# Zero products in front of the expert products' wait, in a streaming encoder step on one core

## Chip, cores and metric

The kernel runs on one core of a Trainium2 chip. The metric is the device time of one execution in microseconds (us), as the median over runs. The program is written engine by engine: TensorE (PE, whose weight loads the profile lists as PEld), VectorE (DVE), ScalarE (ACT), GpSimd (POOL) and SyncE (SP) each have their own instruction list, and semaphores order them.

## What is computed

One inference step of a one-layer trunk over 1,024 prompt tokens and 32 sample tokens, all in fp32, model width 1,024. Cut to what matters here:

```
h  = x + W_out . concat(RMSNorm(StickBreaking(q, k, v)), RMSNorm(SinkWindowGQA(q, k, v)))
h' = h + PEER(RMSNorm(h));   y = RMSNorm(h')

peer_ffn(x):                                   # 8 heads, 16 experts each, of 16384
    q = x @ w_q;  s1 = q1 . keys_1;  s2 = q2 . keys_2
    v1, i1 = top_k(s1, 16);  v2, i2 = top_k(s2, 16)
    best, pos = top_k(v1 + v2, 16);  idx = chosen of i1 * 128 + i2;  gate = softmax(best)
    hid = gelu(u[idx] . x)
    y   = sum_k gate * hid * v[idx]            # rows of u and v are fetched by index
```

Each token fetches 128 rows of u and of v (4 KB each), so the expert rows are nearly all of the traffic from memory.

## The kernel before

The first phase (to about 60 us) projects the first tile of 128 tokens. All the rest is one fused phase, written as a list of slots, `for n in range(FIRST_SLOT, LAST_SLOT)`, which each engine walks in the same order. A slot is one gather: from slot 0 to slot 1,055 POOL starts one indirect DMA (L975) that brings 128 rows of u and v, 8 KB each, into one of the eight places of the ring `uv`. Slots 0 to 1,055 cover 33 groups of 32 tokens.

The work of a slot pair (a batch) passes through four engines. DVE multiplies the u half with the tokens and sums (`dot`, L1195). ACT applies Gelu (L1115) and makes two diagonal matrices of gate times activation, `diag` (L1121); POOL prepares their gate part, `gate_fold` (L961). PE, in slot 2*batch+3, waits for the batch's diagonals and multiplies them with the v half (`experts`, L1733): four products of a 128x32 stationary tile with 512 moving columns, each into its own quarter of the partitions of the PSUM tile `y_acc`. The semaphore `vmm` then counts the gathers whose place in the ring is free, and POOL's gather n waits until n-7 of them are done (`hold(pool, S["vmm"], n - RING + 1)`).

Between these, tables of slots place the other work by hand. `STEP_AT` holds the steps of the stick-breaking attention: PE's `scores` (L1465) in the step's slot, `sums` (L1485, L1488, L1492) four slots later, `values` (L1512) eight slots later, with ACT's softplus and exponential and DVE's `keep` (L1211, L1217) between them. `WINDOW_AT`, `TAIL_AT`, `PRODUCT_AT` hold the window attention and the output projection (L1627), `ROUTE_AT` the routing of one head (queries L1668, L1676, L1682, selection L1703, with the top-k on DVE), `X_AT` the copies of tokens (L1654), `PAIR_AT` the folding of finished groups (L1716). Up to slot 216 or so PE also projects the remaining tokens (L1594). In each slot PE does `experts` first and the other work after it, in program order; nothing on PE overtakes a wait.

`y_acc` has two banks of 512 columns, and a group's products are summed in one of them from its first batch (`opens`, which sets `start=True`) to its last.

Of the kernel before, what the change touches and what calls it, by code (L numbers as in the profile page):

```python
# [13 lines left out]
P = 128  # L14
# [27 lines left out]
GT = 32  # L42
# [47 lines left out]
def hold(engine, sem, value):  # L90

    engine.wait_ge(sem, value)
    engine.nop(nofuse=True)
# [400 lines left out]
def steps_of(t):  # L494

    return 2 * blocks_of(t) if t < NT else blocks_of(t)
# [5 lines left out]
def route_slot(t, head):  # L502

    if t == 0:
        return 8 * head - 23
    if t == 1:
        return 88 + 10 * head
    return t * P - 62 + (14 if t < NT else 10) * head

def stretch(t):

    return 7 if t in STREAMED else 0

def tail_slot(t):

    return route_slot(t, 0) - 28 - stretch(t)

def window_slot(t, w):

    return tail_slot(t) - 20 + 4 * w

def step_slot(t, e):

    return window_slot(t, 0) - 6 - 4 * (steps_of(t) - e)
# [13 lines left out]
LATE_K_AT = {}  # L542
# [4 lines left out]
GATHERS = (NT + 1) * P - 3 * TS  # L547
# [5 lines left out]
STEP_AT = {step_slot(t, e): (t, e) for t in range(NT + 1) for e in range(steps_of(t))}  # L553
WINDOW_AT = {window_slot(t, w): (t, w) for t in range(NT + 1) for w in range(4)}
TAIL_AT = {tail_slot(t): t for t in range(NT + 1)}
TAIL_END_AT = {tail_slot(t) + stretch(t): t for t in range(NT + 1)}
PRODUCT_AT = {tail_slot(t) + 9 + k * (2 if t in STREAMED else 1): (t, k) for t in range(NT + 1) for k in range(DK)}
ROUTE_AT = {route_slot(t, head): (t, head) for t in range(NT + 1) for head in range(PH)}
# [3 lines left out]
PAIR_AT = {min(PT * (g + 1), GATHERS): g for g in range(NP)}  # L562
X_FIRST = [-10, -5, 12, 60, 98, 126, 168, 188]
X_AT = {}
# [3 lines left out]
FINISH_AT = {min((t + 1) * P, GATHERS): t for t in range(NT + 1)}  # L568

def fused_phase(nc, io, r):

    with ExitStack() as ctx:
        def sb(name, shape, dt=F32):
            return ctx.enter_context(nc.sbuf_tensor("f_" + name, shape, dt))
# [3 lines left out]
        w_q, w_out, ident, neg_suffix, neg_ones = r.w_q, r.w_out, r.ident, r.neg_suffix, r.neg_ones  # L579
# [42 lines left out]
        w_first = uv[:, 0:4, :].rearrange("p r (k n) -> p (r k) n", n=DM)  # L622
        w_stream = (part(4, 6), g_final[:])
        hid = sb("hid", [P, 8, 2])
        act_hid = sb("act_hid", [P, 4, 2])
        gate_fold = sb("gate_fold", [P, 3, 2, GT])
        diag = sb("diag", [P, 3, 2, GT])
# [3 lines left out]
        y_acc = ps("y_acc", [P, DM])  # L631
# [52 lines left out]
        def expert_of(n):  # L684

            pair, s = divmod(n, PT)
            head, s = divmod(s, 2 * PART if pair < NP - 1 else PART)
            j, rank = divmod(s, PART)
            g = 2 * pair + j
            return (g, g // GROUPS, g % GROUPS, head, rank)  # L690
# [258 lines left out]

        @block.gpsimd  # L950
        def _(pool):
            nc.gpsimd.memset(q_pad[:], 0.0).then_inc(S["zeroed"], 1)

            def spread_gates(batch):
                g, t, j, head, rank = expert_of(2 * batch)
                hold(pool, S["routed"], t * PH + head + 1)
                if batch >= 3:
                    pool.wait_ge(S["diag"], batch - 2)
                full = [P, 2, GT]
                k = j * PART + rank  # L960
                nc.gpsimd.tensor_tensor(gate_fold[:, batch % 3, :, :], fold[:].unsqueeze(1).broadcast_to(full),  # L961
                                        gates[:, head, k:k + 2].unsqueeze(2).broadcast_to(full),
                                        ALU.mult).then_inc(S["gate_fold"], 1)

            hold(pool, S["op"], 1)
            for n in range(GATHERS):
                if n < RING:
                    hold(pool, S["late_mm"], 2 * n + (2 if n < RING // 2 else 4))
                g, t, j, head, rank = expert_of(n)
                if rank == 0:  # L970
                    hold(pool, S["routed"], t * PH + head + 1)
                if n >= RING:
                    hold(pool, S["vmm"], n - RING + 1)
                k = j * PART + rank
                pool.indirect_dma_start(uv[:, n % RING, :], None, io["peer_uv"],  # L975
                                        bass.IndirectOffsetOnAxis(ap=idx[:, head, k:k + 1], axis=0),
                                        ).then_inc(S_UV[n % RING], 16)
                if n % 2 == 1:
                    spread_gates(n // 2)
# [471 lines left out]
        def _(pe):  # L1451
# [257 lines left out]
            def fold_pair(pair, b, n):  # L1709
# [7 lines left out]
                                            start=True, stop=True, skip_group_check=True)  # L1717
                last.then_inc(S["y_fold"], 1)

            def experts(batch):  # L1720
                g = expert_of(2 * batch)[0]
                opens = 2 * batch == FIRST_OF[g]
                pe.wait_ge(S["diag"], batch + 1)
                if opens and g >= 2:
                    pe.wait_ge(S["y_ev"], g - 1)
                if batch == 0:
                    pe.wait_ge(S["late_ev"], IN_Y)
                    pe.wait_ge(S["late_nat"], sum(u < IN_Y for u in LATE_NATURAL))
                for i in range(2):
                    n = 2 * batch + i  # L1730
                    for b in range(2):
                        quarter = slice((i + 2 * b) * GT, (i + 2 * b + 1) * GT)
                        last = nc.tensor.matmul(y_acc[quarter, g % 2 * 512:(g % 2 + 1) * 512], diag[:, batch % 3, i, :],  # L1733
                                                uv[:, n % RING, DM + b * 512:DM + (b + 1) * 512],
                                                start=opens, stop=False, skip_group_check=True)
                    last.then_inc(S["vmm"], 1)

            for n in range(FIRST_SLOT, LAST_SLOT):
                if n % 2 == 1 and 0 <= n - 3 < GATHERS:
                    experts(n // 2 - 1)  # L1740
# [89 lines left out]
```

## Time and profile before

| | |
|---|---|
| median of 3 runs | 3173.43 us (3172.75 to 3174.1) |
| the profiled execution's own time | 3165.28 us |
| its span, first to last instruction | 3163.4 us |
| PE busy | 2237.8 us, 71% |
| DVE busy | 2204.5 us, 70% |
| ACT, POOL busy | 49% each |
| mean granted TensorE clock | 0.797 of 2.4 GHz |
| moved by DMA | 1216.73 MB, 385 GB/s over the span |

### The profile page before, as it was taken

The page shows a single profiled execution, that of the slowest core. Times are in us where ns is not written, and L with a number is a line of the kernel's source. Part 1 is how long each engine was busy: PE and PEld are TensorE (multiplying, and loading weights), DVE is VectorE, ACT ScalarE, POOL GpSimd, SP SyncE. Part 2 cuts the span into 40 slices and gives each one's busy share as a digit, 9 for nine tenths or more (in the row PEclk, how much of TensorE's full clock was granted, in tenths as well). Part 3 has the DMA queues.
Part 4 walks back from the last instruction along what each step waited for, and adds up shares of the span by engine and source line. Part 5 has one row for each costly group of instructions (what it writes and reads, how often), then busy time and mean ns, then how long its engine had stood idle before and what let it go on. Part 6 is the DMA issues. An engine that isn't in the chain of part 4 may idle for free.

```text
span 3163.4 us, 42434 instructions
## 1 busy us (share of the span) xinstructions
PE 2237.8 (71%) x12346; PEld 1128.1 (36%) x12346; DVE 2204.5 (70%) x5717; ACT 1539.9 (49%) x3399; POOL 1544.9 (49%) x1596
## 2 busy tenths in 40 slices
PE   7978788688767756766577657767677666767663
PEld 4755334344333322332243223332333234432220
DVE  3268548684677767786777766786777767686886
ACT  2235325452257425753476337752677347753222
POOL 0034455354544555455555554455554644466553
PEclk9989889789877867887688778887788877767675
DMA  8379999899999999999999999999999999999997
GB/s 326 95 289 411 417 400 416 322 407 383 421 420 373 417 422 397 363 417 416 420 378 354 417 425 359 364 419 421 394 373 366 423 389 406 406 393 417 426 425 299
DMA packets 243623, 1216.73 MB, mean 385 GB/s; under 512 B 30528, under 2 KB 90304, under 8 KB 107200
## 3 DMA queue, kind: packets, MB, share of 16 engines
q0 software_dynamic: 152528, 1108.81, 85.4%
q1 hardware_dynamic: 90864, 105.22, 9.6%
q8 instruction: 99, 1.62, 0.2%
q14 instruction: 132, 1.08, 0.1%
HBM read 1197.56 MB, written 16.47 MB: 384 GB/s over the span
## 4 chain that ended last, share of the span: by engine, by line
DMA 30%; PE 27%; DVE 20%; issue 8%; DVEq 5%; ACT 3%; POOL 2%; ACTq 2%; SPq 0%; another core or an unknown queue 0%; POOLq 0%
DMA r_uv<-peer_uv,f_idx 27%; DVE r_uv L1195 8%; PE f_y_acc L1733 6%; PE f_q_ps L1668 4%; PE f_z L1627 3%; PE f_z L1485 3%; POOL r_uv L975 2%; PE f_z L1492 2%; PE f_y_acc L1594 2%; PE f_z L1465 2%; ACTq L1119 2%; DMA f_work<-w_out 1%; PE f_o_sb L1512 1%; PE f_o_sw L1654 1%; ACT f_diag L1121 1%
## 5 line engine op out<-in xcount | busy, mean ns | idle before, releaser
L975 POOL DMA_INDIRECT r_uv<-peer_uv,f_idx x1056 | 1270.1, 1203 | 1358.7 <-PE f_y_acc L1733 960.7
L1195 DVE CUSTOM_DVE_ANT_0 r_uv<-r_uv,r_x_rep 128x1024 f32<-128x1024 f32 x1056 | 1287.4, 1226 | 521.0 <-DMA r_uv<-peer_uv,f_idx 511.4
L1733 PE MATMUL f_y_acc<-r_uv,f_diag 128*32 128x512 f32 x4224 | 722.4, 760 | 689.7 <-ACT f_diag L1121 684.5
L1115 ACT ACTIVATE f_act_hid<-f_hid 128x2 f32<-128x2 f32 x528 | 107.3, 203 | 942.7 <-DVE f_hid L1195 916.2
L1733 PEld LDWEIGHTS f_y_acc<-r_uv,f_diag 128*32 128x32 f32 x4224 | 94.7, 119 | 972.1 <-ACT f_diag L1121 893.9
L988 ACT ACT_TABLE_LOAD x191 | 245.1, 1283 | 235.3 <-PE f_z L1465 168.7
L961 POOL TENSOR_TENSOR f_gate_fold<-r_fold,f_gates 128x64 f32<-128x64 f32 x528 | 269.0, 509 | 172.7 <-ACT f_diag L1121 157.3
L1115 ACT ACT_TABLE_LOAD x259 | 332.3, 1283 | 4.5
L1668 PE MATMUL f_q_ps<-r_w_q,f_xnT 128*128 128x256 f32 x1152 | 322.8, 429 | 9.7 <-ACT f_xnT L1084 5.8
L1121 ACT ACTIVATE f_diag<-f_gate_fold,f_act_hid 128x32 f32<-128x32 f32 x1056 | 281.9, 314 | 37.9 <-issue 1.7
L1668 PEld LDWEIGHTS f_q_ps<-r_w_q,f_xnT 128*128 128x128 f32 x1152 | 236.3, 214 | 101.1 <-issue 43.0
L1485 PE MATMUL f_z<-f_work,r_neg_suffix 128*128 128x512 f32 (+2 forms) x178 | 134.0, 847 | 73.6 <-DVE f_work L1217 51.1
L1512 PEld LDWEIGHTS f_o_sb<-f_work 128*128 128x128 f32 (+2 forms) x848 | 104.6, 187 | 20.2 <-ACT f_work L1020 10.2
L1627 PE MATMUL f_z<-r_w_out,f_work 128*128 128x512 f32 (+1 forms) x192 | 100.1, 665 | 13.2 <-DVE f_work L1282 13.2
L1512 PE MATMUL f_o_sb<-f_work 128*128 128x64 f32 (+2 forms) x848 | 105.3, 281 | 2.0 <-ACT f_work L1020 2.0
L1654 PE MATMUL f_o_sw<-r_ident,f_xnT 128*32 128x128 f32 x2112 | 92.5, 329 | 18.9 <-issue 13.7
L1465 PE MATMUL f_z<-f_q_pad,f_work 128*128 128x256 f32 x288 | 89.4, 440 | 16.8 <-DMA f_work<-scratch_projT 16.8
L1485 PEld LDWEIGHTS f_z<-f_work,r_neg_suffix 128*128 128x128 f32 (+1 forms) x178 | 37.8, 257 | 165.7 <-DVE f_work L1217 118.6
L1465 PEld LDWEIGHTS f_z<-f_q_pad,f_work 128*128 128x128 f32 x288 | 67.3, 237 | 78.4 <-issue 72.0
L1654 PEld LDWEIGHTS f_o_sw<-r_ident,f_xnT 128*32 128x32 f32 x2112 | 72.1, 133 | 58.6 <-issue 56.1
L1492 PE MATMUL f_z<-f_work,r_neg_ones 128*128 128x512 f32 (+1 forms) x144 | 91.0, 723 | 0.0
L1195 DVE DVE_READ_ACCUMULATOR2_ANT f_hid<- 128x1 f32 x1056 | 85.7, 81 | 0.0
(209 smaller groups left out, 2964.2 us busy)
## 6 DMA issues: line engine op xcount, KB each, us to landing
r_uv<-peer_uv,f_idx POOLq DMA_INDIRECT x1056
f_work<-scratch_projT SPq DMA_DIRECT2D x86, 128.0 KB
r_w_out<-w_blocks SPq DMA_DIRECT2D x36, 256.0 KB
f_work<-out_sb_v_prompt SPq DMA_DIRECT2D x72, 128.0 KB
r_uv<-w_blocks SPq DMA_DIRECT2D x16, 512.0 KB, 11.0
r_w_q<-w_peer_q SPq DMA_DIRECT2D x8, 1024.0 KB, 10.6
x_in<-x_prompt SPq DMA_DIRECT2D x8, 512.0 KB, 10.0
f_q_pad<-scratch_projT SPq DMA_DIRECT2D x64, 64.0 KB
```

Of the source, the lines that this page charges most:

```text
L961: nc.gpsimd.tensor_tensor(gate_fold[:, batch % 3, :, :], fold[:].unsqueeze(1).broadcast_to(full), gates[:, head, k:k + 2].unsqueeze(2).bro ...
L975: pool.indirect_dma_start(uv[:, n % RING, :], None, io["peer_uv"], bass.IndirectOffsetOnAxis(ap=idx[:, head, k:k + 1], axis=0),).then_inc( ...
L988: act.preload_act_table_set("natural_log_exp_and_others")
L1115: nc.scalar.activation(act_hid[:, batch % 4, :], hid[:, batch % 8, :], ACT.Gelu)
L1121: made = nc.scalar.activation(diag[:, batch % 3, i, :], gate_fold[:, batch % 3, i, :], ACT.Copy, scale=act_hid[:, batch % 4, i:i + 1])
L1195: nc.vector.tensor_tensor_reduce(row_u, row_u, x_rep[:, g % 3, :], 1.0, 0.0, ALU.mult, ALU.add, hid[:, n // 2 % 8, n % 2:n % 2 + 1]).then_ ...
L1465: last = nc.tensor.matmul(z[:, at:at + 256], kT[:, (e % 2) * 256 + m * P:(e % 2) * 256 + (m + 1) * P], q_pad[:, f, m, :, :].rearrange("p a ...
L1485: nc.tensor.matmul(out, neg_suffix[0:keys, 0:keys], sp[0:keys, 0:width], start=False, stop=False, skip_group_check=True)
L1512: last = nc.tensor.matmul(o_sb[0:n, hd * HD:(hd + 1) * HD], probs[0:keys, i * n:(i + 1) * n], block, start=(e == 0 and i == 0), stop=False ...
L1654: last = nc.tensor.matmul(o_sw[c * GT:(c + 1) * GT, k % 4 * P:(k % 4 + 1) * P], xnT[:, k, tokens], ident[:], start=True, stop=True, skip_g ...
L1668: last = nc.tensor.matmul(q_ps[:, 0:2 * QH], xnT[:, k, :], w_q[:, k, head * 2 * QH:(head + 1) * 2 * QH], start=(k == 0), stop=(k == DK - 1))
L1733: last = nc.tensor.matmul(y_acc[quarter, g % 2 * 512:(g % 2 + 1) * 512], diag[:, batch % 3, i, :], uv[:, n % RING, DM + b * 512:DM + (b + ...
```

## The change

A tile of zeros, 128x32, is cleared once by POOL. Before PE waits for a batch's diagonals it now issues a number of products with that zero tile as the stationary operand and `neg_ones`, repeated to 512 columns, as the moving one. They go into the first quarter of the bank in which the batch's group is being summed, so they add nothing. A batch that opens its bank gets none. How many there are is a table made when the program is built: `PE_WORK` adds up a cost in us for PE's work in each slot, and `FILL_AT[n]` is the number of products of cost 0.43 that fill the two slots n-2 and n-1 up to 3.0. It starts at slot 261. In all 590 products stand ahead of 191 of the 528 batches: one at 14 of them, two at 36, three at 60 and four at 81.

```diff
@@ -568,6 +568,25 @@
+PE_WORK = {n: 1.1 for n in range(3, GATHERS + 3, 2)}
+
+
+def count_work(table, offset, cost):
+
+    for slot in table:
+        PE_WORK[slot + offset] = PE_WORK.get(slot + offset, 0.0) + cost
+
+
+for table, offset, cost in ((STEP_AT, 0, 0.9), (STEP_AT, 4, 1.7), (STEP_AT, 8, 0.8), (WINDOW_AT, 0, 0.4), (WINDOW_AT, 4, 0.4),
+                            (WINDOW_AT, 6, 0.4), (TAIL_AT, 6, 0.9), (TAIL_END_AT, 24, 0.9), (PRODUCT_AT, 0, 1.7),
+                            (X_AT, 0, 1.0), (ROUTE_AT, 0, 1.7), (ROUTE_AT, 1, 1.7), (ROUTE_AT, 4, 0.3), (ROUTE_AT, 6, 0.5),
+                            (ROUTE_AT, 15, 0.3), (PAIR_AT, 4, 0.5), (PAIR_AT, 8, 0.5), (LATE_K_AT, 0, 0.9)):
+    count_work(table, offset, cost)
+FILL_TO, FILLER = 3.0, 0.43
+FILL_AT = {n: int((FILL_TO - PE_WORK.get(n - 2, 0.0) - PE_WORK.get(n - 1, 0.0)) / FILLER)
+           for n in range(2 * P + 5, GATHERS + 3, 2)}
@@ -622,6 +641,7 @@
+        zeros = sb("zeros", [P, GT])
@@ -949,6 +969,7 @@
         @block.gpsimd
         def _(pool):
+            nc.gpsimd.memset(zeros[:], 0.0)
             nc.gpsimd.memset(q_pad[:], 0.0).then_inc(S["zeroed"], 1)
@@ -1717,9 +1738,18 @@
+            def fill(n, g):
+
+                for _ in range(FILL_AT.get(n, 0)):
+                    nc.tensor.matmul(y_acc[0:GT, g % 2 * 512:(g % 2 + 1) * 512].rearrange("p (a c) -> p a c", a=4), zeros[:],
+                                     neg_ones[:].unsqueeze(1).broadcast_to([P, 4, P]), start=False, stop=False,
+                                     skip_group_check=True)
+
             def experts(batch):
                 g = expert_of(2 * batch)[0]
                 opens = 2 * batch == FIRST_OF[g]
+                if not opens:
+                    fill(2 * batch + 3, g)
                 pe.wait_ge(S["diag"], batch + 1)
```

The lists below name matmuls by line, output, operands and shape; L1763 of the changed kernel is L1733 of the one before, L1506 is L1485, L1513 is L1492, L1486 is L1465, L1533 is L1512, L1697 is L1676, L1703 is L1682, L1724 is L1703 and L1675 is L1654. The first place is PE's list in a stretch with attention steps, about 1921 to 1948 us of the trace (slots 609 to 615). Before:

```order
L1512 MATMUL f_o_sb<-f_work 128x64 x4
L1733 MATMUL f_y_acc<-r_uv,f_diag 32x512 x4
L1676 MATMUL f_q_ps<-r_ident,f_q 128x128 x2
L1733 MATMUL f_y_acc<-r_uv,f_diag 32x512 x4
L1485 MATMUL f_z<-f_work,r_neg_suffix 128x512
L1492 MATMUL f_z<-f_work,r_neg_ones 128x512
L1465 MATMUL f_z<-f_q_pad,f_work 128x256 x2
L1512 MATMUL f_o_sb<-f_work 128x64 x4
L1682 MATMUL f_q_ps<-r_keysT,f_q 128x128 x2
L1733 MATMUL f_y_acc<-r_uv,f_diag 32x512 x8
L1485 MATMUL f_z<-f_work,r_neg_suffix 128x512
```

The same place in the changed kernel:

```order
L1533 MATMUL f_o_sb<-f_work 128x64 x4
L1763 MATMUL f_y_acc<-r_uv,f_diag 32x512 x4
L1697 MATMUL f_q_ps<-r_ident,f_q 128x128 x2
L1744 MATMUL f_y_acc<-r_neg_ones,f_zeros 32x512 x3
L1763 MATMUL f_y_acc<-r_uv,f_diag 32x512 x4
L1506 MATMUL f_z<-f_work,r_neg_suffix 128x512
L1513 MATMUL f_z<-f_work,r_neg_ones 128x512
L1486 MATMUL f_z<-f_q_pad,f_work 128x256 x2
L1533 MATMUL f_o_sb<-f_work 128x64 x4
L1703 MATMUL f_q_ps<-r_keysT,f_q 128x128 x2
L1763 MATMUL f_y_acc<-r_uv,f_diag 32x512 x4
L1744 MATMUL f_y_acc<-r_neg_ones,f_zeros 32x512 x4
```

Three zero products now stand between the turning of the queries and the next expert products, and four between two batches that followed each other; every other row keeps its place. The second place is PE's list in the last groups, about 3015 to 3030 us of the trace, where no attention is left. Before:

```order
L1733 MATMUL f_y_acc<-r_uv,f_diag 32x512 x4
L1676 MATMUL f_q_ps<-r_ident,f_q 128x128 x2
L1733 MATMUL f_y_acc<-r_uv,f_diag 32x512 x4
L1703 MATMUL f_sel_ps<-f_packed,r_fold 32x8 x4
L1654 MATMUL f_o_sw<-r_ident,f_xnT 32x128 x16
L1682 MATMUL f_q_ps<-r_keysT,f_q 128x128 x2
L1733 MATMUL f_y_acc<-r_uv,f_diag 32x512 x8
```

The same place in the changed kernel:

```order
L1763 MATMUL f_y_acc<-r_uv,f_diag 32x512 x4
L1697 MATMUL f_q_ps<-r_ident,f_q 128x128 x2
L1744 MATMUL f_y_acc<-r_neg_ones,f_zeros 32x512 x3
L1763 MATMUL f_y_acc<-r_uv,f_diag 32x512 x4
L1724 MATMUL f_sel_ps<-f_packed,r_fold 32x8 x4
L1675 MATMUL f_o_sw<-r_ident,f_xnT 32x128 x16
L1703 MATMUL f_q_ps<-r_keysT,f_q 128x128 x2
L1763 MATMUL f_y_acc<-r_uv,f_diag 32x512 x4
L1744 MATMUL f_y_acc<-r_neg_ones,f_zeros 32x512 x4
L1763 MATMUL f_y_acc<-r_uv,f_diag 32x512 x4
```

Here too the zero products come just ahead of expert products, where PE would otherwise go straight to the wait for `diag`.

## Rows read from the trace of the kernel before

**Rows 1.** The page: span, busy times, and the clock in 40 slices.

```profile
span 3163.4 us, 42434 instructions
...
PE 2237.8 (71%) x12346; PEld 1128.1 (36%) x12346; DVE 2204.5 (70%) x5717; ACT 1539.9 (49%) x3399; POOL 1544.9 (49%) x1596
...
PEclk9989889789877867887688778887788877767675
```

**Rows 2.** Stretches: length; PE, PEld, DVE, ACT, POOL busy; clock; DMA share; GB/s.

```profile
967.00:3163.00 2196.00, 1477.67 (x8350) 701.29 (x8342) 1608.78 (x4109) 1170.34 (x2500) 1159.05 (x1190) 0.76 0.97 396
...
1560.00:1680.00 120.00, 86.81 (x502) 44.20 (x502) 85.08 (x212) 92.50 (x154) 57.87 (x59) 0.83 0.94 371
...
2880.00:3120.00 240.00, 143.99 (x775) 57.32 (x773) 190.93 (x514) 76.79 (x217) 142.26 (x147) 0.70 1.01 423
...
1935.00:1955.00 20.00, 11.06 (x49) 4.28 (x42) 18.66 (x54) 15.51 (x26) 9.49 (x10) 0.78 0.94 353
```

**Rows 3.** Waits in 967 to 3163: total us, times, longest.

```profile
POOL r_uv L975 <- PE f_y_acc L1733: 681.1, 277, 9.2
...
PE f_y_acc L1733 <- ACT f_diag L1121: 575.9, 222, 5.3
DVE r_uv L1195 <- DMA r_uv<-peer_uv,f_idx: 357.0, 300, 3.2
```

**Rows 4.** The chain in 967 to 3163: its shares by line.

```profile
by line: DMA r_uv<-peer_uv,f_idx 31.3%; issue 8.9%; DVE r_uv L1195 8.9%; PE f_y_acc L1733 5.9%; PE f_q_ps L1668 3.8%; PE f_z L1485 3.3%; PE f_z L1492 2.1%; POOL r_uv L975 1.9%; PE f_z L1627 1.8%; ACTq L1119 1.8%; PE f_z L1465 1.6%; PE f_o_s
```

**Rows 5.** The chain in 1915 to 1955: start, us, what.

```profile
1915.77 1.06 PE f_y_acc L1733 x8
...
1918.82 0.86 PE f_z L1485 x2
1919.67 0.86 PE f_z L1492 x2
...
1926.88 1.93 PE f_y_acc L1733 x8
1928.81 2.01 PE f_z L1485 x2
1930.82 1.71 PE f_z L1492 x2
```

**Rows 6.** PE's timeline in 1923 to 1953: start, us, group, idle before.

```profile
1923.16 0.44 PE L1676 MATMUL f_q_ps<-r_ident,f_q 128*128 128x128 f32 x2
1926.88 1.93 PE L1733 MATMUL f_y_acc<-r_uv,f_diag 128*32 128x512 f32 x8 [3.28 <-ACT f_diag L1121]
...
1938.96 1.55 PE L1733 MATMUL f_y_acc<-r_uv,f_diag 128*32 128x512 f32 x8 [3.15 <-ACT f_diag L1121]
...
1952.52 1.47 PE L1733 MATMUL f_y_acc<-r_uv,f_diag 128*32 128x512 f32 x8 [3.94 <-ACT f_diag L1121]
```

**Rows 7.** PEld's timeline, the output projection of the sample tokens.

```profile
2864.01 0.18 PEld L1627 LDWEIGHTS f_z<-r_w_out,f_work 128*32 128x32 f32 x1 [0.68 <-issue]
2864.86 0.18 PEld L1627 LDWEIGHTS f_z<-r_w_out,f_work 128*32 128x32 f32 x1 [0.68 <-issue]
...
2870.65 0.11 PEld L1627 LDWEIGHTS f_z<-r_w_out,f_work 128*32 128x32 f32 x1 [0.32 <-issue]
2871.08 0.11 PEld L1627 LDWEIGHTS f_z<-r_w_out,f_work 128*32 128x32 f32 x1 [0.32 <-issue]
```

**Rows 8.** Three short stretches, columns as in rows 2.

```profile
2863.00:2867.80 4.80, 4.64 (x6) 1.06 (x7) 4.32 (x13) 2.42 (x6) 3.01 (x3) 0.50 1.02 430
2867.80:2873.00 5.20, 5.20 (x49) 2.02 (x48) 4.90 (x12) 1.22 (x4) 1.40 (x1) 1.00 1.01 427
...
3076.10:3082.80 6.70, 6.70 (x23) 1.83 (x24) 5.45 (x19) 0.74 (x3) 2.71 (x4) 0.50 1.03 422
```

**Rows 9.** The other clearing on POOL: min, median, max ns, start.

```profile
L952 POOL MEMSET f_q_pad<- x1: 952/952/952, 62.7 to 62.7; 128x1024 f32 x1
```

## Prediction

> **What bounds the kernel now.** I read the page first: the span, the busy times and the clock line [rows 1]. PE is busy 71% of the span, DVE 70%, so no compute engine is full, and the clock line falls from 9 to about 7 after the first third. I therefore took the stretches next, and cut at 967 us, because the table of zero products starts at slot 261, which is reached close behind that time. From 967 to the end [rows 2] PE is busy 1477.67 of 2196 us, the mean clock is 0.76, and the DMA share is 0.97 at 396 GB/s. The reader is to see two kinds of stretch. In 2880 to 3120 the DMA queue is always full (1.01, 423 GB/s) and the clock is lowest (0.70): there the gathers are the bound, and nothing that PE does can show. In 1560 to 1680, where attention steps run, the DMA share is 0.94 at 371 GB/s, with ACT at 92.50 and PE at 86.81 of 120 us: there a chain through the compute engines sets the pace by a little.
>
> The waits after 967 [rows 3] say how they are tied. PE waits 575.9 us in 222 waits for `diag` ahead of its expert products. POOL waits 681.1 us for those products to free a place in the ring, and DVE waits 357.0 us for gathers. It is a loop of eight places, and all of its members wait at some time. The chain [rows 4] gives gathers 31.3%, and PE's six named lines 5.9+3.8+3.3+2.1+1.8+1.6 = 18.5%, which is 406 us of 2196.
>
> What the clock does to that chain stands in one cycle of the attention [rows 5]. At full clock the expert products take 1.06 us and the two sums 0.86 each. Eleven us later the same three take 1.93, 2.01 and 1.71. Between them PE stood idle for 3.28 us ahead of L1733 [rows 6]; it had been at 2.4 GHz before, and the products after that idle time run at 1.2 GHz.
>
> **The change part by part.** *What a zero product costs.* No zero product stands in this trace, but the output projection of the 32 sample tokens has its shape: 128x32 stationary, 512 moving columns, into one quarter of the partitions, one behind the other. Its weight loads follow each other by 0.85 us (2864.01, 2864.86) at half clock and by 0.43 us (2870.65, 2871.08) at full clock [rows 7, 8]. A product is two of them: 0.86 us at 2.4 GHz, 1.70 at 1.2. The table counts 0.43, half of that. So 590 products are 507 us of PE at full clock, and about 1,000 at half. From below the cost can't be nothing, because they stand in PE's list; the expert products overlap four at a time (1.06 us for four), since each has its own quarter, but these all name the same quarter, so I take 0.86.
>
> The Trainium skill ("TensorE: Matmul & The Clock Gate", Part 3, what overlaps and what doesn't) says that a weight load overlaps running matmuls only where its row group is another one, which speaks against this change, since here it is always the same one. By that rule each of the 1,180 halves would cost 0.43+0.11 us with the load time of rows 7, 637 us in all. The spacing of 0.43 with the load inside it [rows 7] says that it is hidden, and the sum goes by 507.
>
> *Where it lies.* The 191 fills stand ahead of the wait that costs 575.9 us in 222 waits, 2.59 us each; a fill has 3.09 products on average, 2.66 us. On average it fits almost exactly, which means that half overhang. In the cycle above [rows 6]: three products (2.58) in 3.28 us fit; four (3.44) in 3.15 overhang by 0.29; four in 3.94 fit. What stands behind an overhang is the batch's expert products and behind them, in PE's order, the next sums and scores; for the products POOL waits (ring), for the sums ACT and DVE. I estimate the mean overhang at full clock at 0.4 us, between 0.29 and the value for a scatter of 1 us around equal means. L1733 is 5.9% of the chain, 130 us, at 1.06 to 1.93 each about 90 passes of the roughly 400 batches after 967; so of 191 fills some 45 lie on the chain: 45 x 0.4 = 18 us lost.
>
> *What it gives.* Would these products keep the clock up? In 2863 to 2867.8 PE did nothing but L1627 in one quarter, at 0.50; from 2867.8 the clock is 1.00 [rows 8]. A dense run of this very shape raised it. A mean clock of 0.76 is half clock for 48% of the time. Of the chain's 406 us on PE that is 195 us at half clock, of which full clock would save 97. The idle time ahead of L1733 is 576 of PE's 718 idle us (2196 - 1477.67), 80%, and the slots just after a tile boundary have few or no products, so I take three quarters of it: 73 us. Less 18 is 55 us shorter on PE's side of the chain.
>
> *What of it arrives.* The DMA queue is idle for 3% of 2196 us, 66 us, so that is about the ceiling, and 2880 to 3120 can't gain at all. And DVE is next in line: behind the slow products of 1926.88 the chain runs through DVE, busy 18.66 of the 20 us in 1935 to 1955 [rows 2]. I take 40% of 55, 22 us, where 0% is the DMA case below and 100% is the bound. The one added clearing on POOL covers a thirty-second of the columns of the one that takes 952 ns [rows 9]: at most 0.9 us, taken as 0.1.
>
> The sum is made against the profiled execution: 3165.28 - 22 = 3143. The median of the runs is 8 us above that execution, so the forecast for a median is 3173.4 - 22 = 3151, which I round to 3152.
>
> **The rivals.** *The fills overhang* (slower). The mechanism is the table's 0.43 for what costs 0.86. Where a fill begins at half clock, four products take 6.8 us against waits of 3 to 4 us. For it speaks the near equality above; against it, that the earlier fills should have kept the clock up. It decides where the mean overhang on the chain's 45 passes exceeds what arrives of the gain, 0.4 x 73 = 29 us: 0.65 us. If half the fills started at half clock, 2.66 us more each, the mean would be 1.3+0.4 = 1.7 us, 77 us lost less 29: +48, a median of 3221. Chance 0.22.
>
> *The zero products don't count for the clock.* Nothing here has an all-zero operand, and not all busy time counts alike: in 3076.1 to 3082.8 PE is busy throughout and stays at 0.50 [rows 8]. Then the fills take 52% x 507 + 48% x 1003 = 745 us, more than PE's 718 idle us: at least 27 us longer, and with the 142 us of idle time that stands elsewhere up to 169: 3200 to 3342. Against it stands the run in one quarter. Chance 0.07. [...]
>
> *The transfers hide it* (no change). DMA share 0.97, and 1.01 where the clock is lowest; what PE saves is then waited for at the ring or at DVE. For it speaks that DVE's and DMA's shares together are above 40% of the chain; against it 371 GB/s in the attention stretches beside 423. It gives 3173 within 6. Chance 0.17.
>
> *Weight loads in the open*, the rule above as a mechanism: 637 us against 576 of waits, 61 us over, 3190 to 3234. The spacing of rows 7 leaves it 0.02.
>
> **How the numbers follow.** Faster through the clock has 0.52, hidden 0.17, overhang 0.22, no count 0.07, open loads 0.02. A measurement of this kernel can tell about 0.2% (6 us) from no change, so faster 0.52, same 0.17, slower 0.31. The likeliest case's own range is 3110 (the DMA ceiling, 66 us, nearly reached) to 3166. The range for 8 in 10 goes on to the overhang's 3221: 3112 to 3222, which leaves out the uncounted case and the ends.
>
> **What the profile would show.** Right: zero products that follow each other by 0.86 us, mean clock after 967 above 0.90, L1733's mean near the 1.06 group in the attention stretches, PE's idle time ahead of L1733 below 150 us, attention stretches above 380 GB/s and 2880 to 3120 unchanged. Overhang: the clock up, but `diag` ready before PE comes, POOL's wait for L1733 above 681 and the attention stretches longer. No count: the clock at or below 0.76 and PE busy above 95%. I would be wrong most simply if the next member of the loop, DVE or ACT, takes the whole gain.

## The result and the profile after

The changed kernel took 3142.89 us (median of 4 runs, 3140.76 to 3144.15) against 3173.09 us before (4 runs): a ratio of 0.9931, 95% interval 0.9911 to 0.9951, 30 us less by the medians. On a second chip the ratio was 0.9912 (0.9885 to 0.9938). The forecast was 3152 with 3112 to 3222. Ratios here and below are of runs in the fast state; one run of e8 (3654 us) and one of e10 (3200 us) are left out of them.

The page of the changed kernel, with the lines that answer to [rows 1], and its group of zero products:

```profile
span 3138.8 us, 44795 instructions
...
PE 2544.2 (81%) x13526; PEld 1189.3 (38%) x13526; DVE 2204.5 (70%) x5717; ACT 1539.3 (49%) x3399; POOL 1544.6 (49%) x1597
...
PEclk8989889798978999899998999899998988899989
...
L1744 PE MATMUL f_y_acc<-r_neg_ones,f_zeros 128*32 128x512 f32 x1180 | 553.5, 607 | 0.0
```

PE does 306 us more than before and the span is 24.6 us shorter. The clock line, which used to fall to 6, 7 and 8 after the first third, now holds 8 and 9 there. The stretches, to be read beside [rows 2]:

```profile
967.00:3138.00 2171.00, 1787.41 (x9530) 765.60 (x9530) 1611.09 (x4117) 1172.70 (x2505) 1162.80 (x1191) 0.92 0.98 401
1560.00:1680.00 120.00, 96.29 (x549) 46.33 (x548) 87.56 (x219) 95.62 (x157) 54.27 (x58) 0.91 0.95 377
...
2880.00:3100.00 220.00, 172.23 (x814) 61.54 (x816) 178.92 (x496) 69.50 (x200) 127.88 (x131) 0.90 1.01 425
```

The mean clock after 967 us went from 0.76 to 0.92, so the part of the time at 1.2 GHz from 48% to 16%, two thirds of it gone. In the last groups (2880 to 3100) the clock rose from 0.71 to 0.90 and the transfers stayed where they were (424 and 425 GB/s, share 1.01): that clock bought nothing. In the attention stretch they rose from 371 to 377 GB/s.

The waits, for [rows 3]:

```profile
POOL r_uv L996 <- PE f_y_acc L1763: 636.5, 276, 9.9
...
DVE r_uv L1216 <- DMA r_uv<-peer_uv,f_idx: 360.2, 315, 3.1
...
PE f_y_acc L1763 <- ACT f_diag L1142: 225.7, 152, 4.4
```

PE waits 350 us less for the diagonals. POOL waits 45 us less for PE's expert products, although PE now does more ahead of the products that free its places.

The same cycle of the attention, on PE's timeline of the changed kernel (start, us, group, idle before), to be read beside [rows 5, 6]:

```profile
1915.58 2.76 PE L1744 MATMUL f_y_acc<-r_neg_ones,f_zeros 128*32 128x512 f32 x6
1918.93 1.06 PE L1763 MATMUL f_y_acc<-r_uv,f_diag 128*32 128x512 f32 x8 [0.59 <-ACT f_diag L1142]
1919.92 1.12 PE L1506 MATMUL f_z<-f_work,r_neg_suffix 128*128 128x512 f32 x2
1920.88 1.02 PE L1513 MATMUL f_z<-f_work,r_neg_ones 128*128 128x512 f32 x2
...
1924.92 3.60 PE L1744 MATMUL f_y_acc<-r_neg_ones,f_zeros 128*32 128x512 f32 x8
1928.65 1.06 PE L1763 MATMUL f_y_acc<-r_uv,f_diag 128*32 128x512 f32 x8
...
1935.42 3.60 PE L1744 MATMUL f_y_acc<-r_neg_ones,f_zeros 128*32 128x512 f32 x8
1939.55 1.07 PE L1763 MATMUL f_y_acc<-r_uv,f_diag 128*32 128x512 f32 x8 [0.53 <-ACT f_diag L1142]
```

The three idle times of 3.28, 3.15 and 3.94 us have become fills of 2.76, 3.60 and 3.60 us with 0.59, none and 0.53 us behind them. The expert products after the first take 1.06 us instead of 1.93, and the two sums 1.12 and 1.02 instead of 2.08 and 1.92 on the same view. From the expert products at 1915.77 to those at 1952.52 before are 36.75 us; the same seven batches now go from 1907.81 to 1939.55, 31.74 us. This cycle is a favourable one: it has nearly all that its stretch of 32 batches gained (slots 579 to 643 in the table below).

Where along the run the time came from is read from the start of the expert products that open every 64 slots, in both traces:

| slots | before, us | changed, us | work beside the experts |
|---|---|---|---|
| 323 to 387 | 178.0 | 176.1 | attention steps of the next tile |
| 387 to 451 | 169.6 | 168.5 | tail, routing |
| 451 to 515 | 183.2 | 180.6 | attention |
| 515 to 579 | 170.1 | 168.0 | tail, routing |
| 579 to 643 | 188.0 | 182.8 | attention |
| 643 to 707 | 167.6 | 170.3 | tail, routing |
| 707 to 771 | 191.1 | 183.6 | attention |
| 771 to 835 | 166.6 | 168.0 | tail, routing |
| 835 to 899 | 190.1 | 180.6 | attention |
| 899 to 963 | 169.6 | 169.7 | tail, routing |

The five attention stretches gave 26.7 us in this pair of traces, and the five others together took 1.0 us more than before. The trace of the same kernel on the second chip, set against the same trace of before, has 20.5 us less in the attention stretches and 1.8 more in the others. The rise from tile to tile isn't in it (1.9, 3.8, 8.2, 2.6, 4.0), so only the split between the two kinds of stretch is to be relied on.

### The profile page after: what moved, and what is told of

Same layout as the page of the kernel before. It is cut to its first block, busy times and chain, and to the rows that moved or that the text cites. A ratio compares the mean times of both kernels' runs of the same rounds, so it can differ in the third digit from the quotient of the medians.

```text
span 3138.8 us, 44795 instructions
## 1 busy us (share of the span) xinstructions
PE 2544.2 (81%) x13526; PEld 1189.3 (38%) x13526; DVE 2204.5 (70%) x5717; ACT 1539.3 (49%) x3399; POOL 1544.6 (49%) x1597
## 4 chain that ended last, share of the span: by engine, by line
DMA 31%; PE 25%; DVE 22%; issue 8%; DVEq 5%; ACT 3%; ACTq 2%; POOL 1%; SPq 0%; POOLq 0%
DMA r_uv<-peer_uv,f_idx 27%; DVE r_uv L1216 8%; PE f_y_acc L1763 5%; PE f_z L1648 3%; PE f_q_ps L1689 3%; PE f_z L1506 2%; PE f_y_acc L1615 2%; PE f_z L1513 2%; PE f_z L1486 2%; POOL r_uv L996 1%; DMA r_w_out<-w_blocks 1%; ACTq L1140 1%; PE f_o_sb L1533 1%; DMA f_work<-scratch_projT 1%; DVE f_work L1238 1%
## 5 line engine op out<-in xcount | busy, mean ns | idle before, releaser
L1763 PE MATMUL f_y_acc<-r_uv,f_diag 128*32 128x512 f32 x4224 | 675.7, 651 | 343.1 <-ACT f_diag L1142 342.0
L1744 PE MATMUL f_y_acc<-r_neg_ones,f_zeros 128*32 128x512 f32 x1180 | 553.5, 607 | 0.0
L982 POOL TENSOR_TENSOR f_gate_fold<-r_fold,f_gates 128x64 f32<-128x64 f32 x528 | 265.8, 503 | 191.1 <-ACT f_diag L1142 175.7
L1763 PEld LDWEIGHTS f_y_acc<-r_uv,f_diag 128*32 128x32 f32 x4224 | 106.3, 111 | 629.1 <-ACT f_diag L1142 515.6
L1689 PE MATMUL f_q_ps<-r_w_q,f_xnT 128*128 128x256 f32 x1152 | 309.0, 415 | 9.5 <-ACT f_xnT L1105 5.1
L1689 PEld LDWEIGHTS f_q_ps<-r_w_q,f_xnT 128*128 128x128 f32 x1152 | 226.4, 205 | 88.1 <-issue 33.8
L1744 PEld LDWEIGHTS f_y_acc<-r_neg_ones,f_zeros 128*32 128x32 f32 x1180 | 123.6, 112 | 339.8 <-issue 334.8
L1506 PE MATMUL f_z<-f_work,r_neg_suffix 128*128 128x512 f32 (+2 forms) x178 | 115.1, 735 | 90.7 <-DVE f_work L1238 64.0
L1533 PEld LDWEIGHTS f_o_sb<-f_work 128*128 128x128 f32 (+2 forms) x848 | 97.9, 176 | 20.4 <-ACT f_work L1041 10.3
L1533 PE MATMUL f_o_sb<-f_work 128*128 128x64 f32 (+2 forms) x848 | 97.8, 267 | 4.8 <-ACT f_work L1041 4.8
L1486 PE MATMUL f_z<-f_q_pad,f_work 128*128 128x256 f32 x288 | 88.3, 436 | 16.3 <-DMA f_work<-scratch_projT 16.3
L1506 PEld LDWEIGHTS f_z<-f_work,r_neg_suffix 128*128 128x128 f32 (+1 forms) x178 | 32.9, 224 | 160.4 <-DVE f_work L1238 115.9
L1675 PE MATMUL f_o_sw<-r_ident,f_xnT 128*32 128x128 f32 x2112 | 79.4, 294 | 16.4 <-issue 14.3
L1486 PEld LDWEIGHTS f_z<-f_q_pad,f_work 128*128 128x128 f32 x288 | 65.4, 230 | 71.6 <-issue 60.0
L1615 PE MATMUL f_o_sw<-r_w_out 128*128 128x384 f32 (+1 forms) x224 | 83.4, 507 | 6.7 <-DMA r_w_out<-w_blocks 4.8
```

The costliest lines, as they stand in the source:

```text
L1486: last = nc.tensor.matmul(z[:, at:at + 256], kT[:, (e % 2) * 256 + m * P:(e % 2) * 256 + (m + 1) * P], q_pad[:, f, m, :, :].rearrange("p a ...
L1506: nc.tensor.matmul(out, neg_suffix[0:keys, 0:keys], sp[0:keys, 0:width], start=False, stop=False, skip_group_check=True)
L1533: last = nc.tensor.matmul(o_sb[0:n, hd * HD:(hd + 1) * HD], probs[0:keys, i * n:(i + 1) * n], block, start=(e == 0 and i == 0), stop=False ...
L1689: last = nc.tensor.matmul(q_ps[:, 0:2 * QH], xnT[:, k, :], w_q[:, k, head * 2 * QH:(head + 1) * 2 * QH], start=(k == 0), stop=(k == DK - 1))
L1744: nc.tensor.matmul(y_acc[0:GT, g % 2 * 512:(g % 2 + 1) * 512].rearrange("p (a c) -> p a c", a=4), zeros[:], neg_ones[:].unsqueeze(1).broad ...
```

## The experiments

Every ratio is against the kernel before on the same chip and comes with its 95% interval; the clock and PE's wait for `diag` are those of 967 to 3120 us, where the kernel before has 0.77 and 558.4 us and the changed one 0.92 and 225.3.

| run | products | clock | wait, us | ratio |
|---|---|---|---|---|
| changed kernel | 590 | 0.92 | 225.3 | 0.9931 (0.9911 to 0.9951) |
| changed kernel, second chip | 590 | 0.92 | 233.7 | 0.9912 (0.9885 to 0.9938) |
| e1, 32 rows | 590 | 0.79 | 112.0 | 1.0355 (1.031 to 1.04) |
| e10, 64 rows | 590 | 0.88 | 176.1 | 1.0034 (1.0004 to 1.0063) |
| e7, 128 columns | 590 | 0.92 | 216.7 | 0.9908 (0.9884 to 0.9933) |
| e2, attention half only | 275 | 0.84 | 400.1 | 0.9942 (0.9917 to 0.9967) |
| e3, other half only | 315 | 0.84 | 400.7 | 0.9985 (0.9967 to 1.0003) |
| e4, table with 0.86 | 258 | 0.85 | 387.0 | 0.9963 (0.995 to 0.9977) |
| e11, up to 3.43 | 820 | 0.94 | 120.7 | 0.9901 (0.9879 to 0.9923) |
| e5, up to 3.86 | 1073 | 0.97 | 50.3 | 1.0039 (1.0018 to 1.006) |
| e8, behind the experts | 546 | 0.90 | 373.9 | 1.0062 (1.0038 to 1.0085) |
| e6, opening batches too | 678 | 0.95 | 169.2 | 0.9916 (0.9885 to 0.9946) |
| e9, from slot 5 | 654 | 0.92 | 229.1 | 0.9918 (0.9892 to 0.9944) |

**Is it the clock?** The same products at the same places, with 32 rows of the array at work instead of 128:

```diff
-nc.tensor.matmul(y_acc[0:GT, ...], zeros[:],
-                 neg_ones[:].unsqueeze(1).broadcast_to([P, 4, P]), ...
+nc.tensor.matmul(y_acc[0:GT, ...], zeros[0:32, :],
+                 neg_ones[0:32, :].unsqueeze(1).broadcast_to([32, 4, P]), ...
```

> Edit: the same 590 zero products at the same places, but with 32 of the 128 rows of the array in use instead of 128. Their time on PE should be the same 0.86 us at full clock (moving columns set it), so the overhang is the same or larger; only what they do for the clock can differ. Theory 1 (the gain of 30 us comes through the granted clock, and the clock goes by how much of the array is at work): the clock after 967 us falls from 0.92 to near 0.76, the products take up to 1.7 us each, and the kernel is slower than before, 3190 to 3300 us. Theory 2 (any issued product keeps the clock up): clock 0.92 and 3143 within 6 us. Theory 3 (the gain is not the clock but the later expert products, which shift the order of the transfers): clock near 0.76 and still near 3143 us.

The clock stayed at 0.79 and the kernel took 3.55% longer than before. Its group on the page:

```profile
L1744 PE MATMUL f_y_acc<-r_neg_ones,f_zeros 32*32 32x512 f32 x1180 | 696.9, 734 | 0.0
```

and PE's timeline in an attention stretch:

```profile
1923.78 4.58 PE L1744 MATMUL f_y_acc<-r_neg_ones,f_zeros 32*32 32x512 f32 x6
1928.29 1.93 PE L1763 MATMUL f_y_acc<-r_uv,f_diag 128*32 128x512 f32 x8
...
1934.60 3.62 PE L1744 MATMUL f_y_acc<-r_neg_ones,f_zeros 32*32 32x512 f32 x8
1939.15 1.93 PE L1763 MATMUL f_y_acc<-r_uv,f_diag 128*32 128x512 f32 x8 [0.94 <-ACT f_diag L1142]
```

The three products of the first fill take 4.58 us instead of 2.76, because part of them runs at half clock; the wait behind them is gone, and the expert products still take 1.93 us. The second fill runs at full clock, four products in 3.62 us as with 128 rows, and still the expert products behind it take 1.93 us. So the same products, where they don't hold the clock up and therefore run partly at half clock themselves, cost this program some 110 us. Theory 3, that a shift in the order of transfers gives the gain, gets no support: these products shift the expert products too, by more, since they run longer. A shift of just the changed kernel's length without the clock was not tried. Half the rows:

```diff
+nc.tensor.matmul(y_acc[0:GT, ...], zeros[0:64, :],
+                 neg_ones[0:64, :].unsqueeze(1).broadcast_to([64, 4, P]), ...
```

> Edit: the 590 products with 64 of the 128 rows in use. With 128 rows the clock after 967 us is 0.92 and the ratio 0.993, with 32 rows 0.79 and 1.035. If the clock goes by the rows in use: between the two, clock 0.82 to 0.88, ratio 1.00 to 1.02. If there is a step between 32 and 64: the same as the changed kernel.

It lies between: clock 0.88 and 1.0034, with runs from 3147 to 3200 us. Its trace says where it loses. The five attention stretches take 925.9 us against 930.4 before and the five others 849.2 against 843.5, but from slot 1027 to the end it takes 118.0 us against 91.7. A window there, and one of its fills:

```profile
3119.00:3159.00 40.00, 40.00 (x84) 6.64 (x83) 11.24 (x20) 3.68 (x15) 5.13 (x6) 0.50 0.48 197
...
3129.18 7.03 PE L1744 MATMUL f_y_acc<-r_neg_ones,f_zeros 64*32 64x512 f32 x8
```

PE is busy for the whole 40 us and the clock stays at 0.50; four products take 7.03 us, and PE, which waits for nothing, is now the bound. In its attention stretches four of them take 3.62 us and the expert products behind them 1.06, at full clock. In these two places, then, 64 rows held a full clock and did not bring back one that was lost. The mean of 0.88 hides both. And all the columns of the array instead of a quarter:

```diff
-nc.tensor.matmul(y_acc[0:GT, ...], zeros[:], ...
+nc.tensor.matmul(y_acc[:, ...], zeros[:, 0:1].broadcast_to([P, P]), ...
```

> Edit: the same products with a stationary operand of 128 columns (zeros) instead of 32, so that all of the array is at work and not a quarter of its columns. Same moving columns, so the same 0.86 us; the weight loads take 0.19 instead of 0.11 us and should stay hidden. If columns in use count for the clock as rows do: the clock after 967 us rises from 0.92 to 0.96 or more, ratio to before 0.990. If they don't (as the projection of the sample tokens in one quarter suggests): clock 0.92 and the same time as the changed kernel within 0.2%.

Clock 0.92 as with 32 columns, ratio 0.9908, not told apart from the changed kernel (0.9912 on the same chip). Its weight loads are longer and still lie under the running product:

```profile
1912.26 0.19 PEld L1744 LDWEIGHTS f_y_acc<-r_neg_ones,f_zeros 128*128 128x128 f32 x1 [0.24 <-issue]
1912.69 0.19 PEld L1744 LDWEIGHTS f_y_acc<-r_neg_ones,f_zeros 128*128 128x128 f32 x1 [0.24 <-issue]
```

**Where does it pay?** The products in only one half of each 128 slots:

```diff
-           for n in range(2 * P + 5, GATHERS + 3, 2)}
+           for n in range(2 * P + 5, GATHERS + 3, 2) if n % P >= P // 2}     # e3: < P // 2
```

> Edit: the zero products stand only in the second half of each 128 slots, where the attention steps of the next tile run: 275 of 590. Theory 1 (the gain arises where the compute chain sets the pace): all of the gain, 3143 within 6 us, and if anything a few us less, since in the stretch from 643 to 707 the changed kernel took 2.7 us longer than before. Theory 2 (the clock helps everywhere, the stretches only move the gain): about half, 3157 us.

> Edit: the other half, the zero products only in the first half of each 128 slots: 315 of 590. Theory 1 (there the gathers set the pace): 3173 within 6 us, although the clock in those slots rises to about 0.9. Theory 2: about half of the gain, 3157 us.

The attention half alone gave 0.58%, the other half 0.15% with an interval that reaches no change, at the same mean clock of 0.84. The interval of e2 holds both of its theories, all of the gain and half of it; that of e3 leaves out the half. So the same rise of the clock is worth more where the compute chain sets the pace, which agrees with the table of the stretches. How many times more stays open, since the two intervals touch.

**How long should a fill be?** Three runs change one number of the table:

```diff
-FILL_TO, FILLER = 3.0, 0.43
+FILL_TO, FILLER = 3.0, 0.86       # e4
+FILL_TO, FILLER = 3.43, 0.43      # e11
+FILL_TO, FILLER = 3.86, 0.43      # e5
```

> Edit: the cost of a product in the table is 0.86 instead of 0.43, which is what it takes at full clock. So 258 products at 177 places instead of 590 at 191. Overhang theory (the doubled length costs more than it gives): faster than the changed kernel, ratio to before 0.988 to 0.992, with the clock after 967 us at 0.87 or so. Clock theory (the clock's gain grows with the length, and the overhang of the changed kernel is small): about half of the clock's rise, 0.84, and half of the gain, ratio 0.996.

> Edit: the two slots filled up to 3.43, so one product more at every place than in the changed kernel, 820 in all instead of 590; 1073 gave 1.004. If the cost of overhang begins at once: ratio 0.996 to 1.000. If the changed kernel's length isn't the best yet: 0.989 to 0.992, with the clock after 967 us at 0.95.

> Edit: the two slots are filled up to 3.86 by the table instead of 3.0, so one or two products more stand at every place, 1073 instead of 590. Theory 1 (overhang costs about 0.86 us for each product beyond the wait wherever the compute chain runs): PE near 95% busy or more, PE's wait for diag near zero, slower than the changed kernel by 40 to 150 us, 3180 to 3290 us, in spite of a clock of 0.97 or more. Theory 2 (the loop has slack of about a microsecond per slot pair in most places, so that one product more costs nothing): within 10 us of 3143.

With the true cost in the table (258 products) more than half of the gain is lost, 0.9963 beside 0.9912 on the same chip, as the clock theory had it: correcting the number would have been a step back. One product more at each place, and one at 39 places that had none (820 in all), gave 0.9901, the lowest of all, though its interval overlaps that of the changed kernel. Two more, and one or two at 75 places that had none (1,073), cost it all: 1.0039. PE's timeline of e5 shows six products (twelve records, the last of them among those of the expert products) and no wait behind them:

```profile
1936.30 1.07 PE L1763 MATMUL f_y_acc<-r_uv,f_diag 128*32 128x512 f32 x8
1937.19 4.88 PE L1744 MATMUL f_y_acc<-r_neg_ones,f_zeros 128*32 128x512 f32 x11
1941.48 0.63 PE L1763 MATMUL f_y_acc<-r_uv,f_diag 128*32 128x512 f32 x3
1941.91 0.59 PE L1744 MATMUL f_y_acc<-r_neg_ones,f_zeros 128*32 128x512 f32 x1
1941.94 1.42 PE L1763 MATMUL f_y_acc<-r_uv,f_diag 128*32 128x512 f32 x5
```

PE is busy 2041 of 2153 us, and POOL's wait for its products is 757.2 us instead of 636.5. I had expected 40 us at least over the changed kernel; from its ratios of 0.9931 and 0.9912 to 1.0039 it is 34 to 40 us. The turning point lies between one and two products more, when the wait left in front of the experts is nearly used up (120.7 us at e11, 50.3 at e5). On the chain of e5 (967 to 3120) the zero products stand first:

```profile
by line: PE f_y_acc L1744 32.1%; PE f_y_acc L1763 11.6%; DMA r_uv<-peer_uv,f_idx 8.6%; PE f_q_ps L1689 6.4%; issue 4.3%; DVE r_uv L1216 4.3%; PE f_z L1648 4.0%; PE f_z L1506 2.7%; PE f_o_sb L1533 2.2%; PE f_z L1513 2.0%; PE f_z L1486 1.8%; 
```

The stretches say where it loses. In its trace the five attention stretches take 896.6 us, less than before (930.4) and than in the changed kernel (903.7); the five others take 867.5 against 843.5 before, and from slot 963 to the end it takes 270.3 us against 253.1. In such another stretch (2380 to 2554) PE is busy 167.74 of 174 us. So the long fills hurt in the stretches in which the clock buys nothing, and a table with long fills in the attention halves and short ones elsewhere was not tried.

**Does the place matter?** The same products right behind the batch's expert products:

```diff
-                if not opens:
-                    fill(2 * batch + 3, g)
                 pe.wait_ge(S["diag"], batch + 1)
...
                     last.then_inc(S["vmm"], 1)
+                if not opens and 2 * batch + 1 != LAST_OF[g]:
+                    fill(2 * batch + 3, g)
```

> Edit: the same products right behind the batch's expert products instead of ahead of the wait for its diagonals, so they delay the sums, scores and queries that follow in PE's list by their whole length instead of lying in idle time; 546 of the 590 (none behind a bank's last batch). Theory 1 (the place in the idle time is what makes them cheap): the clock still rises to 0.9, but ACT and DVE get their inputs 2.6 us later wherever a fill stands, and the time goes above the kernel before: ratio 1.00 to 1.03. Theory 2 (only the clock matters; PE catches up in the idle time that is left): ratio 0.991 to 0.995.

The clock rose to 0.90, and the kernel was 0.62% slower than before. On its timeline the idle time ahead of the experts is still there, and the fill delays the sums:

```profile
1936.13 1.94 PE L1761 MATMUL f_y_acc<-r_uv,f_diag 128*32 128x512 f32 x8 [3.28 <-ACT f_diag L1142]
1937.84 3.36 PE L1744 MATMUL f_y_acc<-r_neg_ones,f_zeros 128*32 128x512 f32 x6
1941.13 1.12 PE L1506 MATMUL f_z<-f_work,r_neg_suffix 128*128 128x512 f32 x2
```

The clock falls in the 3.28 us and the expert products run at half clock. The sums run at full clock again, but the zero products, 3.36 us long, stand in front of these sums. Its five attention stretches take 951.4 us against 930.4 before.

**Is there more?** Two extensions. Products at the batches that open a bank, where about 3 us of idle time were left:

```diff
+for n in range(2 * P + 5, GATHERS + 3, 2):
+    if n % (P // 2) in (3, 7) or n % P == 23:
+        FILL_AT[n] = 3
...
+                if opens and g >= 2:
+                    pe.wait_ge(S["y_ev"], g - 1)
+                fill(2 * batch + 3, g, opens)      # start=opens
                 pe.wait_ge(S["diag"], batch + 1)
```

> Edit: three products also ahead of the wait at the batches that open a bank (slots 3 and 7 of every 64, where PE still idles about 3 us in the changed kernel) and in slot 23 of every 128 (3.1 us idle). At an opening batch the wait for the evicted bank stands ahead of them and they start the sum with zeros. If idle time that fits a fill is enough, the few us that the queue of transfers idles near the tile boundary shrink: ratio to the kernel before 0.989 to 0.992, 3 to 12 us under the changed kernel. If only the attention stretches count: the same as the changed kernel within 0.2%.

and the table from slot 5 on (`range(5, GATHERS + 3, 2)`):

> Edit: the table starts at slot 5 instead of slot 261, which adds 64 products in the stretch where PE also projects the remaining tokens. If the clock's gain holds there too (half clock for a quarter of that stretch): 1 to 4 us under the changed kernel, ratio 0.990 to 0.992. If the overhang outweighs it where PE is fuller: 0.993 to 0.996.

Neither can be told from the changed kernel: 0.9916 beside 0.9912 on the same chip, though the clock rose to 0.95; and 0.9918, on a chip on which the changed kernel did not run. Of the opening batches, half lie in the half of the slots that e3 had priced at little or nothing, and the others stand ahead of their tile's first attention step; why the idle time there is worth nothing was not looked into. So the lowest ratio is that of e11, with a lead over the changed kernel that these runs don't settle.

## Why the prediction was right, step by step

**A product costs 0.86 us, not the table's 0.43.** Right. The fills of three and four products take 2.76 and 3.60 us with the tail of the last one, and the 1,180 halves follow each other by 0.43 us at full clock. The weight loads lie under the running products, as [rows 7] had it, even with 0.19 us (e7); the Trainium skill's rule ("TensorE: Matmul & The Clock Gate", Part 3, what overlaps and what doesn't), that loads overlap only with another row group, doesn't hold in these traces.

**They keep the clock up.** Right, and shown by e1: the products with 32 rows leave the clock at 0.79 and lose 3.55%. In the timelines above PE's work behind a fill runs at full clock where it ran at half. I had taken that three quarters of the half-clock time would go; it was two thirds (48% to 16%). The rival "they don't count" was wrong for this form and nearly right for the one with 32 rows (0.79 beside 0.77 without any), and its price of 27 to 169 us brackets what e1 cost, 3.55% or some 110 us. I had rested it on the values being zero; what decided was the rows.

**The fills lie in the idle time ahead of the experts.** Right: 576 us of waiting became 226, and e8 shows that the same products elsewhere lose. I had said that less than 150 us would remain, which was too bold. Read batch by batch, the wait at the 191 places with a fill fell from 466 us to 74; the other 150 us stand at batches without one, 60 of them at batches that open a bank. The mean of 2.59 us per wait had mixed the two kinds.

**Overhang of 18 us.** Its size is open. That about half of the fills overhang was right: behind 107 of the 191 PE finds `diag` ready (no wait over 0.1 us). What it costs is not measured by itself. e11 puts 230 products more, nearly all in the same places, and doesn't lose, but its clock is higher too (0.94), so that shows only that the two balance. Zero products do stand on the chain of the changed kernel: under 1.4% in its own trace, 31 us at most, and 2.0% in the second chip's, 43 us. That bounds the overhang from above, since part of that time would have been a wait anyway, and 18 lies within it. The rival was wrong at this length and right at 1,073 products, where the kernel is 34 to 40 us slower than the changed one (ratios of 0.9931 and 0.9912). At that length the zero products hold a third of the chain.

**What it gives on PE's side, and what arrives.** The chain of the changed kernel, for [rows 4] (its shares are of the same 2196 us):

```profile
by line: DMA r_uv<-peer_uv,f_idx 29.9%; DVE r_uv L1216 10.4%; issue 8.5%; PE f_y_acc L1763 4.7%; PE f_z L1648 2.8%; PE f_q_ps L1689 2.6%; PE f_z L1506 2.4%; PE f_z L1513 1.8%; POOL r_uv L996 1.6%; PE f_z L1486 1.4%; DVE f_work L1238 1.4%; P
```

The six lines of PE have 15.7%, 345 us, where they had 406: 61 us less, for which I had put 73. In the trace of the second chip it is 35 us (17.2% of 2153 against 18.8%), so the size is uncertain. The expert line of DVE has 10.4% instead of 8.9%, 33 us more: the next member of the loop took part of the gain, as I had said it could.

I put 22 us of 55; the medians give 30, the two profiled executions 24.5 (3165.28 to 3140.76). My 40% was a choice between two bounds and rests on no reading, so that the time came out near the forecast is in part luck: of 61 us it would be 40 to 49%, but of 61 less 18 of overhang 57 to 70%. What it stood for was right: e2 and e3 together with the stretches show that the gain is made in the attention stretches, and the last stretch at 1.01 DMA share gained nothing. Two smaller marks failed: I had named 380 GB/s for attention stretches, and 1560 to 1680 shows 377; and PE's wait was to fall below 150 us. The 3151 of the sum was put down as 3152, which changes nothing.

## What to carry to other kernels

Where TensorE idles for a few us ahead of a wait and the granted clock is down in the work behind it, filler products in that idle time can pay, but only if that work is on the chain: look first at the DMA share and at what each stretch waits for. Put the filler ahead of the wait and not behind the work, let it use all rows of the array, and find its length by trying, one kind of stretch at a time; here 44% of the products gave about 40% of the gain and 1.8 times as many gave a loss, and the nominal cost in the table was no guide.

## What the runs showed of the hardware

- With the same 590 products in the same places, the mean granted clock after 967 us was 0.92 with 128 rows, 0.88 with 64 and 0.79 with 32. With 128 rows it was 0.92 both for 32 and for 128 columns of the stationary operand.
- Products whose stationary operand is all zeros count for the clock: 0.77 without and 0.92 with them.
- With 64 rows PE was busy for 40 us without a gap (3119 to 3159 of e10) and the clock stayed at 0.50; the changed kernel has 1.00 in its last groups (3078 to 3118).
- The rows in use don't change the time of a product at full clock: four products take 3.62 us with 64 rows (e10) and with 32 (e1), and 3.60 with 128.
